# Second scan by groups: silu written by ScalarE in one pass, and the products of tokens and dt moved from VectorE to GpSimd

## What is computed

```python
xb = silu(centred_dwconv(xb, ma_conv_w, ma_conv_b, rows))         # x and B
cm = silu(centred_dwconv(cm, ma_conv_w, ma_conv_b, rows))         # C, grid tokens only
y_f, h_f = ssd_chunk_scan(xh, dt_f, a[0], bm, cm, s_init[2])      # forward over the tokens
y_b, h_b = ssd_chunk_scan(flip(xh), flip(dt_b), ...)              # and backward
y = y_f + flip(y_b) + xh * ma_d
yz = rms_norm(y * silu(z)) * ma_norm_w
# within a chunk: y += (C B^T * decay) (x * dt); across chunks: the state S, decayed and read by C
```

## Time and profile before

| | before |
|---|---|
| median of the runs | 3715.37 us |
| profiled execution, span from first to last instruction | 3716.2 us |
| mean granted TensorE clock | 0.956 |
| TensorE matmul busy | 3393.3 us (91%) |
| VectorE busy | 2590.8 us (70%) |
| ScalarE busy | 1619.0 us (44%) |
| GpSimd busy | 643.4 us (17%) |
| `ssd_groups` in the trace | from about 1371 to about 2042 us, some 79.3 us for each group in the middle |

### The profile page before, as it was taken

How to read it: one execution, slowest core, us unless ns; L and a number is a source line. 1 busy time by engine, 2 the same in 40 slices (tenths; PEclk the granted TensorE clock), 3 DMA queues, 4 the chain that set the end, 5 groups by cost and what they waited for, 6 DMA issues and landing times. The chain is left out here.

```text
span 3716.2 us, 48906 instructions
## 1 busy us (share of the span) xinstructions
PE 3393.3 (91%) x18596; PEld 2933.3 (79%) x18596; DVE 2590.8 (70%) x4394; ACT 1619.0 (44%) x2678; POOL 643.4 (17%) x417
## 2 busy tenths in 40 slices
PE   7989998998999978888896999899798999999997
PEld 3868987865889877777775787599797788999997
DVE  2646875344878767877776244499996787888887
ACT  3433432324555544555555232333465434444444
POOL 0211100000433321111111000255200111222220
PEclk9979999998999989999998999999899999999999
DMA  5101100341111111111110424344267998999994
GB/s 213 36 23 51 35 29 31 116 188 46 46 48 50 46 36 46 46 46 46 52 46 22 143 102 164 122 136 136 98 210 240 380 350 334 345 347 338 347 348 155
DMA packets 151320, 519.68 MB, mean 140 GB/s; under 512 B 19008, under 2 KB 64944, under 8 KB 131248
## 3 DMA queue, kind: packets, MB, share of 16 engines
q1 hardware_dynamic: 132656, 382.33, 29.0%
q0 software_dynamic: 18432, 134.23, 9.8%
HBM read 473.22 MB, written 43.28 MB: 139 GB/s over the span
## 5 line engine op out<-in xcount | busy, mean ns | idle before, releaser
L350 PE MATMUL ps<-hT_high,ring_twin 128*128 128x384 f32 (+1 forms) x1768 | 696.9, 394 | 68.0 <-DVE ring_twin L3169 35.5
L352 PE MATMUL ps<-hT_high,ring_twin 128*128 128x384 f32 (+1 forms) x1768 | 650.3, 368 | 0.0
L351 PE MATMUL ps<-hT_low,ring_twin 128*128 128x384 f32 (+1 forms) x1696 | 623.0, 367 | 0.0
L350 PEld LDWEIGHTS ps<-hT_high,ring_twin 128*128 128x128 f32 x1768 | 344.0, 195 | 123.4 <-DVE ring_twin L3169 41.1
L352 PEld LDWEIGHTS ps<-hT_high,ring_twin 128*128 128x128 f32 x1768 | 343.3, 194 | 32.9
L351 PEld LDWEIGHTS ps<-hT_low,ring_twin 128*128 128x128 f32 x1696 | 330.9, 195 | 29.9 <-issue 2.9
L350 PE MATMUL ps<-ex_vh,ex_al 128*128 128x512 f32 x768 | 300.4, 391 | 20.3 <-DVE ex_al L2731 20.3
L2586 POOL DMA_INDIRECT ex_uv<-in_peer_uv,rows_at x128 | 173.0, 1352 | 838.1 <-DVE ex_acc L2690 570.4
L351 PE MATMUL ps<-ex_vl,ex_ah 128*128 128x512 f32 x768 | 301.1, 392 | 0.0
L352 PE MATMUL ps<-ex_vh,ex_ah 128*128 128x512 f32 x768 | 301.1, 392 | 0.0
L2252 POOL TENSOR_TENSOR pr_wl<-pr_w,pr_wh 128x1024 fp32r<-128x1024 f32 x54 | 137.3, 2544 | 468.9 <-ACT pr_wh L2311 468.9
(11 more groups left out here) (605 smaller groups left out, 8002.2 us busy)
## 6 DMA issues: line engine op xcount, KB each, us to landing
ex_v<-in_peer_uv SPq DMA_DIRECT2D x128, 512.0 KB
ex_u<-in_peer_u SPq DMA_DIRECT2D x68, 512.0 KB, 8.1
pr_w<-in_peer_u SPq DMA_DIRECT2D x60, 512.0 KB, 3.6
ring<-in_w_in_ma SPq DMA_DIRECT2D x48, 512.0 KB
gates_by_expert<-sg_gbuf SPq DMA_DIRECT2D x6, 4096.0 KB, 14.6
ex_g<-gates_by_expert SPq DMA_DIRECT2D x32, 768.0 KB, 8.5
ring<-in_w_in_hg SPq DMA_DIRECT2D x40, 512.0 KB, 3.7
ring<-in_w_merge SPq DMA_DIRECT2D x36, 512.0 KB, 3.9
```

The source lines that it names most:

```text
L350: pe.matmul(out, a[1], b[0], start=start, stop=False)
L351: pe.matmul(out, a[0], b[1], start=False, stop=False)
L352: return pe.matmul(out, a[0], b[0], start=False, stop=stop)
```

## The change

ScalarE applies Silu where it applied Sigmoid (x, B, C and z), raises `x_ready` and `zs_ready` itself, and loads the table set of silu in place of that of sigmoid; z is done in place by one instruction of 1024 columns in place of two of 512 into y. VectorE's products `opened` and `opened_z` are gone, and with them the semaphore `sig_ready`. The product `timed` goes from VectorE to GpSimd, over the four grid chunks (1024 columns) and no longer over all six (1536), into one buffer for each direction. GpSimd issues the one of direction 0 at the start of the group and the one of direction 1 between its instructions of step 0 and step 1.

```diff
-        xdt, xw = sb("ma_xdt", [P, NC, 2 * P]), sb("ma_xw", [P, NC, 2 * P])
+        xdt, xw = sb("ma_xdt", [P, 2, NXC, 2 * P]), sb("ma_xw", [P, NC, 2 * P])
 # GpSimd
+                def timed(g, dr):
+                    if dr == 0:
+                        pool.wait_ge(t_copied, 6 * g + 4)
+                    if g > 0:
+                        pool.wait_ge(y_done, 2 * NXC * (g - 1) + NXC * (dr + 1))
+                    pool.tensor_tensor(heads(xdt[:, dr]), heads(xtok[:, C0:NC]),
+                                       over(dt[:, C0:NC, dr, J * g:J * g + J], NXC), ALU.mult).then_inc(xdt_ready, 1)
+
                 for g in range(G):
+                    timed(g, 0)
                     for s in range(2 * NXC):
+                        if s == 1:
+                            timed(g, 1)
 # TensorE
-                            pe.matmul(o, xdt[:, C0 + c, hs], L[:, i % 2, j, :], start=(s == 0), stop=False)
+                            pe.matmul(o, xdt[:, dr, c, hs], L[:, i % 2, j, :], start=(s == 0), stop=False)
 # ScalarE
-                        act.activation(cols(cT[:]), by_col(cv[:, 1, NCTX:T]), ACT.Sigmoid).then_inc(sig_ready, 1)
+                        act.activation(cols(cT[:]), by_col(cv[:, 1, NCTX:T]), ACT.Silu).then_inc(x_ready, 1)
-                    act.activation(to[:, 0:NCTX], cv[:, j % 2, 0:NCTX], ACT.Sigmoid)
-                    act.activation(cols(to[:, NCTX:T]), by_col(cv[:, j % 2, NCTX:T]), ACT.Sigmoid).then_inc(sig_ready, 1)
+                    act.activation(to[:, 0:NCTX], cv[:, j % 2, 0:NCTX], ACT.Silu)
+                    act.activation(cols(to[:, NCTX:T]), by_col(cv[:, j % 2, NCTX:T]), ACT.Silu).then_inc(x_ready, 1)
 # ScalarE, opened_z
-                    if g > 0:
-                        act.wait_ge(ss_done, g)
-                    for e in range(2):
-                        act.activation(y[:, e, :], z[:, g % 2, e, :], ACT.Sigmoid).then_inc(sig_ready, 1)
+                    act.activation(z[:, g % 2], z[:, g % 2], ACT.Silu).then_inc(zs_ready, 1)
-                act.preload_act_table_set("sigmoid_and_others")      # at all three places
+                act.preload_act_table_set("silu_and_others")
 # VectorE: opened, opened_z and timed with all their calls
-                def opened(g, j):
...
-                def timed(g, dr):
...
 # VectorE, skipped
                     dve.wait_ge(zs_ready, g + 1)
+                    if g > 0:
+                        dve.wait_ge(ss_done, g)
```

More of the change, by code:

```diff
@@ L3358, in ssd_groups @@
         heads = lambda a: a.rearrange("p c (h e) -> p c h e", e=MA_P)
-        over = lambda a: a.unsqueeze(3).to_broadcast([P, NC, J, MA_P])
+        over = lambda a, n=NC: a.unsqueeze(3).to_broadcast([P, n, J, MA_P])
         by_col = lambda a: a.rearrange("p (r w) -> p w r", w=GRID_W)
@@ L3363, in ssd_groups @@
         SLOT = (8, 8, 8, 7, 6, 5, 3, 3)
-        sig_at = lambda g, j: 6 * g + j + 1 if j > X1 or g == 0 else 6 * g + j - 1
-        sig_z = lambda g: 6 * g + 8 if g + 1 < G else 6 * g + 6
-        with core.stage("w_in*2", "const_in", "high_ready", "low_ready", "lot_done", "evicted", "conv_done", "sig_ready",
+        with core.stage("w_in*2", "const_in", "high_ready", "low_ready", "lot_done", "evicted", "conv_done",
                         "x_ready", "t_done", "t_copied", "cb_done", "cbm_ready", "sums_done", "lc_ready", "ex_ready",
@@ L3372, in ssd_groups @@
                         "stored", "steps", "asteps") as (
-                block, w_in, const_in, high_ready, low_ready, lot_done, evicted, conv_done, sig_ready,
+                block, w_in, const_in, high_ready, low_ready, lot_done, evicted, conv_done,
                 x_ready, t_done, t_copied, cb_done, cbm_ready, sums_done, lc_ready, ex_ready,
@@ L3691, in _ @@
                         if s == 5:
-                            act.preload_act_table_set("sigmoid_and_others")
+                            act.preload_act_table_set("silu_and_others")
                             if not last:
@@ L3841, in _ @@
                 low(4)
-                opened(0, X0)
                 conv(0, B)
                 low(5)
-                opened(0, X1)
                 conv(0, C)
@@ L3850, in _ @@
                     weighted(g, 0)
-                    opened(g, B)
-                    opened(g, C)
                     if g > 0:
@@ L3856, in _ @@
                     masked(g)
-                    timed(g, 0)
                     low(n + X1)
@@ L3871, in _ @@
                             states(g, 1)
-                            timed(g, 1)
                         if not last and s in (3, 4):
                             conv(g + 1, X1, (s - 3,))
[L3875 to L3879, removed]
                         if not last and s in (5, 6):
```

3 lines of the change are left out of this document (removed).

## The result

The changed kernel takes 3664.48 us (median of four runs, 3662.98 to 3666.18) against 3715.95 us (four runs) on the same chip. The ratio is 0.9858, its 95% interval 0.9844 to 0.9872. On a second chip it was 3661.41 against 3715.18 us, ratio 0.9855 (0.9839 to 0.9872). The forecast was 3680 us, with 3664 to 3700. The direction and the places were right and the gain was 1.4 times the forecast one. The ratio times the 3715.37 us of the forecast gives 3662.6 us, just outside the range.

A forecast was written before the change was run, and what follows sets the result against it. VectorE was taken to hold TensorE up in the first and third window of a group, with ScalarE the next bound. Terms 25.9 + 6.5 + 1.5 + 2.0 = 35.9 us off 3715.4 gave 3680 us, range 3664 to 3700.

The forecast's parts named there:

- VectorE's row is the bound from step 4 to 7, and ScalarE's the next: Second half of a group: VectorE loses 6.7 us, ScalarE then limits; 3.7 us gained a group, 25.9 us over seven.
- the second part of B's convolution: Before step 7, on VectorE: meets GpSimd's `ce` in its middle, stalling up to 1.27 us; 0 to 0.4 us goes back.
- The start of a group: First part of a group: products leave VectorE, states start earlier; 1.0 us gained a group, 6.5 us in all.
- A new wait of about 1 us: TensorE at the last `added` of the states: waits for the third state, delayed by GpSimd's second `timed` holding the port.
- the whole remaining price of the port: GpSimd and VectorE exclude each other; without this lock the first part would gain 2.0 us a group, some 7 us more overall.
- the wait at step 4: TensorE's 2.64 us wait in the second half of a group, slow clock behind it; claimed to go once `timed` leaves VectorE.
- the wait of 2.03 us at the states: TensorE at a group's start, at the third `added`, behind `timed` and a `low` on VectorE; claimed to go.
- Silu: ScalarE's silu in place of sigmoid: taken to cost the same, so nothing in the sum.
- Start and end: Before the first group 1.5 us gained as X0's product goes; with the last group 2.0 us (1.4 to 4).
- The last group: B's product goes before TensorE's transposes and states come earlier; 2.0 us taken, 1.4 to 4.
- more than that: Rival, chance 0.14: the port costs little, gains of 2.0 and 4.0 us a group, 47 in all, time 3668.

The follow-up runs named there:

- the silu half alone: Kernel before with ScalarE writing silu and VectorE's products gone, tokens times dt staying on VectorE with one buffer: 3684.81 us against 3711.29, ratio 0.9926.

## Why the prediction was wrong, point by point

- **VectorE's row is the bound from step 4 to 7, and ScalarE's the next.** Right. From the start of step 3's output to that of step 7 group 3 took 24.68 us and takes 20.60: 4.1 us where I took 3.7 and said 3.6 to 4.0. I had the second part of B's convolution collide with `ce` for longer than before; with `attended` it takes 4.73 us, where it took 4.76. This term of the sum was 0.4 us a group too small, 2.7 us in all.
- **The start of a group.** The step that failed by size is "A new wait of about 1 us: the last `added` starts at 1677.0". The wait is 0.29 us. The mechanism was right, as the timelines show. I took GpSimd's product at 2.4 us from a subtraction with two full inputs; it takes 2.08 us among the states and 1.90 where nothing is in its way, which was the lower end that I had kept. It also starts 0.49 us earlier than I had it. TensorE gains 1.7 us a group here and not 1.0: some 4.4 us over groups 1 to 6. The product left out shows the whole remaining price of the port in groups 1 to 7 as 3.1 us in the stage; the prediction's was 7.
- **One group was taken for all.** This is the step that was missing. The prediction had the slow clock only behind the wait at step 4 and took group 3's 79.3 us for each group. Two of the six, groups 2 and 4, took 80.8. The waits at the states and at step 4 were the same in all six. The difference is where the clock fell. In groups 1, 3, 5 and 6 it fell behind step 4, in groups 2 and 4 behind the wait of 2.03 us at the states, and in no group behind both. Windows of TensorE in the kernel before, behind the wait at the states in group 2 and group 3, and behind that at step 4 in group 2, where group 3 has 0.64:

```profile
1595.60:1599.70 4.10, 4.10 (x15) 3.69 (x14) 3.04 (x9) 0.00 (x0) 0.00 (x0) 0.59 0.41 128
1676.40:1679.00 2.60, 2.60 (x16) 2.46 (x15) 2.40 (x7) 0.00 (x0) 0.00 (x0) 1.00 0.61 202
1635.40:1640.20 4.80, 4.80 (x36) 4.13 (x37) 4.66 (x8) 3.66 (x6) 0.00 (x0) 1.00 0.00 0
```

  Behind one wait of 2.03 us the granted clock is 0.59, a mix of the 1.2 and the 2.4 GHz level, and the same fifteen or sixteen matmuls take 1.5 us longer; behind the other it is 1.00. Behind step 4 the slow clock cost nothing: from step 3's output to step 7's all seven groups take 24.6 to 24.7 us, with it or without it, because VectorE's row is the bound there (in group 2, TensorE then waits 2.90 us at step 6 in place of 0.45). At the states nothing hides it. With the waits gone the clock stays at 1.00 in all of groups 1 to 6, and every group takes 73.5 us. That is 3.0 us which the prediction did not have. Why one wait is followed by the slow clock and another not, no run here tells, and with one trace of the kernel before it is open whether other executions have the same two long groups.
- **Silu.** Right at nothing: 1.12 us for 512 strided columns where sigmoid took 1.11, and 1.04 us for z in one instruction. The sentence that the prediction drew on (the Trainium skill, page "ScalarE: Activation LUTs", section "What ACT_TABLE_LOAD costs": one cost for every function) agrees with these rows for silu, and the table load takes 1.28 us for it.
- **Start and end.** At the start VectorE's product gave the 1.5 us foretold (the wait went from 7.44 to 6.00 us); another 1.0 us came from the filler behind this wait, where the clock was 0.72 and is 0.80. The last group was the term with the least working: 2.0 taken, 4.85 measured. The waits in its first part cost their own length and a clock of 0.85 in 34.5 us; that window is now 28.3 us long at 1.00. From step 3's output to step 7's 1.4 us go back (16.6 us in place of 15.2): the clock is 0.71 there where it was 0.81, and the wait for ScalarE before `rows_of(7)` is 3.44 us in place of 2.87. The text had 4 us as the upper end.
- **The shares.** The rival "more than that", at 0.14, was nearest: it had 3668 us, and its reason (the port costs little) is half of the truth. The forecast's mistakes were all on one side: 2.7 us in steps 4 to 7, 4.4 at the start of groups 1 to 6 and 0.8 in group 0, 3.0 by the clock, 0.9 before the first group and 2.9 in the last, 14.7 of the 14.8 us that were missing.

## What to carry to other kernels

Look at more than one pass of a loop before multiplying: here two passes of six were 1.5 us longer for a reason that one pass did not show. A wait of 2 to 3 us on TensorE can cost more than its length, by a slower clock behind it: 1.5 us at the states in two groups of six and nothing in the others, and nothing at step 4 as long as another engine's row hid it. Once that row was shorter (the silu half alone), the same slow clock behind the same wait cost 0.9 to 2.2 us. And where a product is moved to another engine together with a second buffer, try the buffers and the new place on the old engine: here that gave as much as GpSimd did, since the product only had to leave a place where VectorE was late.

## What the runs showed of the hardware

GpSimd's product of two inputs in which one is repeated over 64 columns takes 1.90 us for 1024 columns where nothing is in its way, and 2.08 us where it starts beside a scaling of the state on VectorE; the subtraction of two full tiles of this size takes 2.36 at least. VectorE and GpSimd excluded each other at every meeting of instructions with two inputs in SBUF that was read here, and where GpSimd had two products back to back, VectorE got one such instruction in between. Two waits of TensorE that were taken away, of 0.29 and 1.01 us, had cost 0.54 and 1.24 us, so each cost some 0.25 us more than its idle time in the trace.
